# Eighteen more panels of a fused first block by seven products of 128x128x128 instead of eight

## The reference

```
def ssd_shortconv_layer_mixer(x, w_in, conv_w, conv_b, dt_bias, a_log, d_skip, norm_w, sc_conv_w, w_out):
    proj = x @ w_in
...
    return jnp.concatenate([y_ssd.astype(x.dtype), y_sc.astype(x.dtype)], axis=-1) @ w_out
...
    for i in range(DEPTH):
...
        x = layer_norm(ALPHA * x + mix.astype(x.dtype), ln_mix_g[i], ln_mix_b[i])
        x = layer_norm(ALPHA * x + swiglu(x, w_ffn_gate[i], w_ffn_up[i], w_ffn_down[i]), ln_ffn_g[i], ln_ffn_b[i])
        gate = jax.nn.sigmoid(x @ w_ple_gate[i] + b_ple_gate[i])
        x = x + (p[i] @ w_ple[i]) * gate
```

## Time and profile before

| | |
|---|---|
| median of 3 runs (range) | 2324.86 us (2323.5 to 2327.66) |
| the profiled execution's own time | 2325.58 us |
| its span, first to last instruction | 2323.8 us |
| mean granted clock of PE | 0.995 |
| PE busy | 2219.6 us, 96% |
| DVE, POOL, ACT busy | 925.1, 435.6, 382.6 us |

### The profile page before, as it was taken

How to read it: one execution, slowest core, us unless ns; L and a number is a source line. 1 busy time by engine, 2 the same in 40 slices (tenths; PEclk the granted TensorE clock), 3 DMA queues, 4 the chain that set the end, 5 groups by cost and what they waited for, 6 DMA issues and landing times. The chain is left out here.

```text
span 2323.8 us, 35156 instructions
## 1 busy us (share of the span) xinstructions
PE 2219.6 (96%) x14569; PEld 1515.7 (65%) x14569; DVE 925.1 (40%) x1969; ACT 382.6 (16%) x857; POOL 435.6 (19%) x365
## 2 busy tenths in 40 slices
PE   8999999999999998998999999999999999989997
PEld 7888899987799987877633333333333333368786
DVE  4242465645444564626333333333333333352322
ACT  2210121024201023225200000000000000023331
POOL 0120498820088850012000000000000000000000
PEclk9999999999999999999999999999999999999999
DMA  6334754465855454323699999999999999953322
GB/s 264 129 123 145 240 173 162 155 235 179 325 204 166 162 182 171 111 110 146 254 427 427 427 428 428 428 429 408 427 428 427 429 428 428 428 210 131 127 80 84
DMA packets 61011, 619.37 MB, mean 267 GB/s; under 512 B 6784, under 2 KB 8064, under 8 KB 12288
## 3 DMA queue, kind: packets, MB, share of 16 engines
q1 hardware_dynamic: 59184, 611.08, 66.3%
q10 hardware_dynamic: 1712, 6.63, 0.9%
HBM read 616.63 MB, written 1.05 MB: 266 GB/s over the span
## 5 line engine op out<-in xcount | busy, mean ns | idle before, releaser
L2958 PE MATMUL ps<-expert_ring,moe_xg 128*64 128x512 f32 x1280 | 282.1, 593 | 9.9 <-DMA expert_ring<-we_dram 9.5
L3001 PE MATMUL ps<-expert_ring,mix_y 128*64 128x512 f32 x1024 | 228.6, 596 | 10.8 <-DMA expert_ring<-we_dram 10.8
L2958 PEld LDWEIGHTS ps<-expert_ring,moe_xg 128*64 128x64 f32 x1280 | 90.3, 137 | 190.6 <-issue 167.3
L466 PE MATMUL ps<-x_res,ring 128*128 128x256 f32 x896 | 201.1, 382 | 8.8 <-DMA x_res<-x_dram 8.8
L466 PEld LDWEIGHTS ps<-x_res,ring 128*128 128x128 f32 x896 | 169.6, 192 | 33.1 <-DMA ring<-w_in_dram 8.7
L3260 DVE TENSOR_SCALAR mix_y<-ps 128x512 f32<-128x512 f32 x32 | 22.1, 692 | 421.5 <-PE ps L2958 421.5
L2774 POOL COPY unscaled_x<-modulations 128x8 f32<-128x8 f32 x1 | 0.2, 198 | 936.6 <-POOLq L3057 936.6
L2958 PE MATMUL ps<-ring,moe_xg 128*64 128x512 f32 x768 | 168.2, 593 | 0.5 <-DVE moe_xg L2919 0.3
L3001 PEld LDWEIGHTS ps<-expert_ring,mix_y 128*64 128x64 f32 x1024 | 69.8, 137 | 147.2 <-issue 127.5
L466 PE MATMUL ps<-third_h,ring 128*128 128x256 f32 x704 | 160.0, 383 | 1.3 <-DVE third_h L3833 1.0
L625 POOL TENSOR_TENSOR seven_weights<-ring 128x512 f32<-128x512 f32 (+1 forms) x72 | 94.1, 1306 | 326.0 <-DVE seven_x_turned L641 289.2
(11 more groups left out here) (625 smaller groups left out, 3317.7 us busy)
## 6 DMA issues: line engine op xcount, KB each, us to landing
expert_ring<-we_dram SPq DMA_DIRECT2D x144, 2048.0 KB, 22.5
ring<-we_dram SPq DMA_DIRECT2D x48, 2048.0 KB, 24.5
ring<-w_in_dram SPq DMA_DIRECT2D x55, 1024.0 KB, 4.9
ring<-ffn_up_dram SPq DMA_DIRECT2D x44, 1024.0 KB, 5.0
ring<-ada_dram SPq DMA_DIRECT2D x36, 1024.0 KB, 4.9
ring<-w_out_dram SPq DMA_DIRECT2D x16, 1024.0 KB, 4.9
ring<-ffn_dn_dram SPq DMA_DIRECT2D x16, 1024.0 KB, 4.9
ring<-ple_g_dram SPq DMA_DIRECT2D x8, 1024.0 KB, 6.5
```

Source lines behind the costliest of these rows:

```text
L466: mm = pe.matmul(core.ps[:, bank_of[n, c], 0:TOK], w[:, k * PANEL + c * P:k * PANEL + c * P + P], sources[panel](k0 + k), start=(k0 + k == ...
L2958: mm = pe.matmul(ps[out, bank, :], xg[:, j % 4, j // 4, :], w[:, bank * D + at:bank * D + at + 512], start=False, stop=(j == 7))
L3001: mm = pe.matmul(ps[out, 2, :], hidt[:, at_k:at_k + S], w[:, i * D + at:i * D + at + 512], start=False, stop=(k == DT - 1))
```

## The change

Eighteen panels become fast: seven pairs of the input linear (6 to 9, which are z's, and 19 to 21, b's last three), pairs 1 to 3 of the mixer's output linear (two panels each) and pairs 1 to 5 of query, key and value. A linear can now name its fast pairs (`only`). In detail:

- `turn` can run on any engine. The turned x of the input linear is made by POOL at the start (`turn_input`); that of the mixer's output linear by DVE behind tile 43 (`turn_mixed`, twice four operations, into memory of `h_turned`); that of query, key and value by DVE behind tile 119 (`turn_added`).
- POOL's part of the heads has one step for each head from slot 20 on, so that `sums` of panels 6 to 9 stand ahead of them and those of 19 to 21 behind.
- The norm's take of tiles 2 to 5 no longer scales x by ALPHA (`kept`), since `keep` has.

```diff
 def takes(self, name, j):
-        return name in self.first_pair and j >= self.first_pair[name]
+        return name in self.first_pair and j >= self.first_pair[name] and (name not in self.only or j in self.only[name])
...
     def gpsimd(pool):
+        for _ in range(FIRST + 1):
+            yield
         pool.wait_ge(cbm_ready.sem, cbm_ready.at(1))
...
-        yield
+            yield
...
-            if m < 6 and self.alpha != 1.0 and not self.split:
+            if m < 6 and self.alpha != 1.0 and not self.split and m // 2 not in self.kept:
...
+FAST_IN, FAST_OUT = (6, 7, 8, 9, 19, 20, 21), (1, 2, 3)
...
+        out_turned = h_turned[:, :, :, :].rearrange("p c w n -> p (c w n)")[:, 0:2 * 4 * (DT // 2) * P].rearrange(
+            "p (g c w n) -> p g c w n", g=2, c=4, n=P)
+
+        def turned_y(product, k0, p):
+            return out_turned[:, k0 // DT, {5: 0, 7: 1, 6: 2, 4: 3}[product], p, :]
...
+        parts_fast |= {"w_in": (FAST_IN[0], turned_x, None, groups("w_in"), FAST_IN), "qkv": (1, turned_x, None, groups("qkv")),
+                       "w_out": (FAST_OUT[0], turned_y, norms[0].keep, groups("w_out"))}
...
+        def turn_input(pool):
+            clear(pool)
+            pool.wait_ge(core.sem_f.sem, core.sem_f.at(16))
+            seven.turn(pool, seven.groups["w_in", 0], core.x[:, 0:4, :], core.x[:, 4:8, :], *(x_turned[:, i, :, :] for i in (0, 2, 1, 3)))
+
+        def turn_mixed(dve):
+            yield WOUT0 - 1
+            for t in range(WOUT0 - DT, WOUT0):
+                core.wait_tile(dve, t)
+            seven.turn(dve, seven.groups["w_out", 0], y_sc[:, 0:4, :], y_sc[:, 4:8, :], *(out_turned[:, 0, i, :, :] for i in (0, 2, 1, 3)))
+            xd_ready(dve, DT - 1)
+            seven.turn(dve, seven.groups["w_out", DT], xd[:, 0:4, :], xd[:, 4:8, :], *(out_turned[:, 1, i, :, :] for i in (0, 2, 1, 3)))
+
+        def turn_added(dve):
+            yield QKV0 - 1
+            dve.wait_ge(run.x_added.sem, run.x_added.at(DT))
+            seven.turn(dve, seven.groups["qkv", 0], core.x[:, 0:4, :], core.x[:, 4:8, :], *(x_turned[:, i, :, :] for i in (0, 2, 1, 3)))
...
-        linear(core, parts, None, tiles, head=head, act_work=more_loads, pool_work=clear, banks=3,
+        linear(core, parts, None, tiles, head=head, act_work=more_loads, pool_work=turn_input, banks=3,
```

More of the change, by code:

```diff
@@ L575, in __init__ @@
         self.first_pair, self.moving_of, self.keepers = {}, {}, {}
-        for name, (first, moving, keeper, groups) in parts.items():
+        self.only = {}
+        for name, (first, moving, keeper, groups, *only) in parts.items():
             self.first_pair[name], self.moving_of[name], self.keepers[name] = first, moving, keeper
+            if only:
+                self.only[name] = only[0]
             for k0, n in groups.items():
@@ L630, in sums, with turn @@
         pool.tensor_tensor(s4, a12, s2, ALU.subtract).then_inc(summed.sem, 1)
-    def turn(self, dve, n, upper, lower, t1, t2, t3, t4):
+    def turn(self, eng, n, upper, lower, t1, t2, t3, t4):
         turned = self.turned
         b11, b12, b21, b22 = upper[:, :, 0:P], upper[:, :, P:TOK], lower[:, :, 0:P], lower[:, :, P:TOK]
-        dve.tensor_tensor(t1, b12, b11, ALU.subtract).then_inc(turned.sem, 1)
-        dve.tensor_tensor(t3, b22, b12, ALU.subtract).then_inc(turned.sem, 1)
-        dve.wait_ge(turned.sem, turned.at(4 * n + 1))
-        dve.tensor_tensor(t2, b22, t1, ALU.subtract).then_inc(turned.sem, 1)
-        dve.wait_ge(turned.sem, turned.at(4 * n + 3))
-        dve.tensor_tensor(t4, b21, t2, ALU.subtract).then_inc(turned.sem, 1)
+        eng.tensor_tensor(t1, b12, b11, ALU.subtract).then_inc(turned.sem, 1)
+        eng.tensor_tensor(t3, b22, b12, ALU.subtract).then_inc(turned.sem, 1)
+        eng.wait_ge(turned.sem, turned.at(4 * n + 1))
+        eng.tensor_tensor(t2, b22, t1, ALU.subtract).then_inc(turned.sem, 1)
+        eng.wait_ge(turned.sem, turned.at(4 * n + 3))
+        eng.tensor_tensor(t4, b21, t2, ALU.subtract).then_inc(turned.sem, 1)
     def copy_first(self, act, n, one):
@@ L1125, with __init__ @@
 class LayerNorm:
-    def __init__(self, core, run, n, g, b, first, alpha, split, fill):
+    def __init__(self, core, run, n, g, b, first, alpha, split, fill, kept=()):
         self.core, self.run, self.n, self.first, self.alpha, self.fill = core, run, n, first, alpha, fill
@@ L1133, in __init__ @@
         self.sem = dict(zip(names, (*core.shared[28:40], *core.shared[61:63])))
-        self.split = split
+        self.split, self.kept = split, kept
         self.added_before = 0
@@ L1727, in first_block @@
         norms = [LayerNorm(core, run, n, (lambda k, l=l, g=g: core.v(g, l * DT + k)), (lambda k, l=l, b=b: core.v(b, l * DT + k)), first,
-                           alpha, split, mods.fill)
+                           alpha, split, mods.fill, FAST_OUT if first == WOUT0 else ())
                  for n, (g, b, l, first, alpha, split) in enumerate((
@@ L1795, in turned_h @@
             return h_turned[:, {5: 0, 6: 1, 4: 2}[product], k0 // 2 + p, :]
-        turn_order = [("ffn_up0", 0), *(("ffn_dn0", k0) for k0 in range(0, FF_T, KG)), ("ple_g0", 0),
+        out_turned = h_turned[:, :, :, :].rearrange("p c w n -> p (c w n)")[:, 0:2 * 4 * (DT // 2) * P].rearrange(
+            "p (g c w n) -> p g c w n", g=2, c=4, n=P)
+        def turned_y(product, k0, p):
+            return out_turned[:, k0 // DT, {5: 0, 7: 1, 6: 2, 4: 3}[product], p, :]
+        turn_order = [("w_in", 0), ("w_out", 0), ("w_out", DT), ("ffn_up0", 0), *(("ffn_dn0", k0) for k0 in range(0, FF_T, KG)), ("ple_g0", 0), ("qkv", 0),
                       ("ffn_up1", 0), *(("ffn_dn1", k0) for k0 in range(0, FF_T, KG)), ("ple_g1", 0)]
@@ L1821, in turn_h @@
             return program
-        turns = [turn_x("ffn_up0", UP0, norms[0]), turn_h("ffn_dn0", UP0), turn_x("ple_g0", PG0, norms[1]),
+        turns = [turn_mixed, turn_added, turn_x("ffn_up0", UP0, norms[0]), turn_h("ffn_dn0", UP0), turn_x("ple_g0", PG0, norms[1]),
                  turn_x("ffn_up1", UP1, norms[2]), turn_h("ffn_dn1", UP1), turn_x("ple_g1", PG1, norms[3])]
```

## The result

| | before | after |
|---|---|---|
| median (range), 5 runs each | 2327.58 us (2323.5 to 2330.14) | 2336.19 us (2332.43 to 2340.84) |
| the profiled execution's own time | 2325.58 us | 2332.43 us |
| its span | 2323.8 us | 2330.6 us |
| granted clock of PE, mean over that execution | 0.995 | 0.993 |
| PE busy | 2219.6 us | 2212.9 us |

The ratio is 1.0039, 95% interval 1.0025 to 1.0053: slower by 0.25 to 0.53%. The forecast was 2328.9 us with a range of 2321 to 2334, and the median of 2336.19 lies above that range. In ten more runs, beside 27 of the kernel before, the ratio was 1.0033 (1.0020 to 1.0045). The saved work is there, and so are the waits. This is the list of PE's waits in the first 640 us of the changed kernel (total, times, longest), cut at three places; it answers to the earlier trace rows.

A forecast was written before the change was run, and what follows sets the result against it. PE, busy 96% at nearly full clock, bounds the kernel. Saved work of 11.8 us against new waits gave +2.3, one clock fall +1.7: +4.0 on 2325.6 is 2329.6, less 0.7 is 2328.9 us; range 2321 to 2334.

The forecast's parts named there:

- The gain, 18 panels at 6.25 us: In all three linears, 18 panels drop from 6.91 to 6.254 us each, saving PE 11.8 us.
- (a): Input linear, pair 9: PE waits for DVE's copy of the state before the spread, 1.5 us.
- (b): b's last tile: the reciprocal delays panel 21's combining, so PE waits for tile 43, 0.7 us.
- (c): Slot 49, output linear: PE's sum of `ln_offset` waits for DVE's take and addition, slowed by POOL, 2.9 us.
- (d): Slot 51, output linear's norm: the squares' reduction starts later, shifting PE's L1195 and all behind it by 4.0 us.
- (e): Attention: scores, weighing and turning wait for tile 124, ACT's copies and DVE's shift and normalising, together 5.0 us.
- the clock term: PE's clock falls to half once for the new waits at slots 49 and 51 together, adding 1.7 us.
- my own price: Cost of one clock fall: 3.6 us at 0.53 do the work of 1.9 us, so 1.7 us.
- 0.7 us above the median: The profiled execution lay 0.7 us above its three runs' median, so 2329.6 became 2328.9 us.
- the sum without the clock: Saved panel work against the five new waits, before any clock fall: +2.3 us.
- the clock falls at every long new wait: Rival: falls at slot 49, slot 51 and the attention, 3 x 1.7 us, giving 2332.3 us; chance 0.15.

The follow-up runs named there:

- in_only: Kernel before with only the input linear's seven panels made fast: 2322.87 us, ratio 0.9987 to the kernel before.
- warm: Changed kernel plus 13 unread matmuls filling PE's waits at slots 49 and 51: 2330.97 us, ratio 1.0017 to the kernel before.
- shift: Kernel before plus nine unread matmuls at slot 49, making later work start 3.9 us later: 2329.93 us, ratio 1.0011.
- split: Changed kernel with the output linear's layer norm in the down projections' form (first sum over four tiles, squares reduced at slot 49): 2325.28 us, ratio 0.9989.
- out_split: Kernel before with only the output linear's six panels fast, its layer norm in the down projections' form: 2323.88 us, ratio 0.9990.
- best: Changed kernel with query, key and value ordinary and the output linear's norm in the down projections' form: 2325.55 us, ratio 0.9990 to the kernel before.
- qkv_only: Kernel before with only the five panels of query, key and value made fast: 2329.98 us, ratio 1.0016 to the kernel before.
- out_only: Kernel before with only the output linear's six panels made fast, norm unchanged in form: 2334.03 us, ratio 1.0037 to the kernel before.

## Why the prediction was wrong

The waits, which were most of the text, came out. By its points:

- The gain, 18 panels at 6.25 us, came: the first and fourth stretches are within 0.1 us of the saved work less the waits reckoned for them.
- (a) 1.36 us for 1.5. (b) 0.42 for 0.7; the terms listed there add up to 10.1 and not 9.95, which would have made it 0.8. Both waits are where they were said to be, and `in_only` shows that this part of the change gains.
- (c) 3.15 for 2.9, and for the reason given, DVE slowed by POOL. DVE's timeline of the changed kernel has the take at 1.07 and the addition at 1.37 us while POOL sums for a later panel; the same take at slot 51, with POOL idle, takes 0.42:

```profile
228.40 0.55 DVE L661 TENSOR_TENSOR seven_stage<-seven_part,ps 128x384 f32<-128x384 f32 x1 [1.24 <-PE ps L430]
228.99 1.07 DVE L1161 TENSOR_TENSOR x_res<-x_res,seven_stage 128x256 f32<-128x256 f32 x1
230.09 1.37 DVE L1242 TENSOR_TENSOR ln_offset<-ln_offset,x_res 128x256 f32<-128x256 f32 x1
...
246.95 0.42 DVE L1161 TENSOR_TENSOR x_res<-x_res,seven_stage 128x256 f32<-128x256 f32 x1
```

- (d) The waits are 1.57 + 1.96 = 3.53 us, where PE was to get the squares 4.0 us later than before. That was a little too large, and the wait ahead of L445 gave 0.5 back (0.90 for 1.36), which I had not counted.
- (e) The six new waits are 4.42 us in sum for 5.0, each within 0.2 of its term. The stretch is 1.75 longer for 1.7 reckoned.
- **The step that failed is the clock term: "I take one fall for the two: +1.7".** In both profiles of the changed kernel (c) and (d) have a fall each, and the unchanged second down projection has a third that the kernel before escaped. On the profiled execution, 2332.43 for 2329.6, 2.8 us were missing: one more fall in the stage, 1.7 by my own price, and the 1.4 us of the unchanged part make 3.1, less what (d) and (e) were too large.
- The other 4.5 us of the miss are in the last step, "0.7 us above the median". It carried an offset over from three runs of the kernel before. Against the five runs of the result (median 2327.58) the same execution was 2.0 us below the median, and against the 91 later ones 1.1 below. So 2.7 us of the miss are in the median of before that I started from, and the forecast change was 4.0 us where 8.2 to 8.6 were measured. The rest is the clock again: the profiled run after had 0.993 where the 15 have 0.9918, and their median is 3.3 us above it.

How much is clock in all can be read from the runs. Over 218 runs of these kernels, each kernel's own mean taken off, the time falls by 1.77 us for each 0.001 of mean clock (correlation -0.89). The 91 runs of before and the 15 of after, grouped by clock (medians):

```
clock    0.991   0.992   0.993   0.994   0.995
before   2332.3  2331.6  2329.5  2329.7  2326.6
after    2336.5  2335.7  2332.0  2331.4  2327.7
runs     1, 4    4, 3    10, 2   17, 2   33, 1
```

At one and the same clock the changed kernel is 1 to 4 us slower, though most of these medians of it are of one to three runs. The means of all runs, 2334.98 and 2327.09 us, are 7.9 apart. Of this the difference in clock, 0.9947 - 0.9918 = 0.0029, is 5.1 us by the slope, and 2.7 are left, near what the sum without the clock had said (+2.3). I had put 1.7 for the clock. The 5.1 is an estimate from a correlation; by profile, 2.65 us of it stand in the output linear's stage (`warm`). The rival nearest to it was the second, "the clock falls at every long new wait", at 2332.3 us, and even that is below the measured median; it counted falls of the changed places only.

What is shown: that the output linear's stage pays 2.65 us to two falls, which are gone when its waits are filled (`warm`); that added work of 3.9 us without a wait does not lower the mean clock (`shift`); that without the three waits the stage is back at its old time or 0.9 us under it, and 7 to 8 us below the changed kernel's (`split`, `out_split`, `best`). Not shown is what lowers the clock elsewhere: the attention's short waits bring no fall there, yet `qkv_only` has a mean of 0.9934, and single places of unchanged work fall in one kernel and not in another (`best`). So the cause of the other half of the 5.1 us stays open.

## What to carry to other kernels

When PE is the bound and every panel is made shorter, the work that hung on "one more tile" loses its cover. Look at each place where two woven steps come to stand next to each other, and give the early step a form that needs only older tiles, as the split norm does. Price a new wait of PE with its length and with the clock that it may cost, for the whole program and not only for its place, and take the clock from many runs, not from one profile. A part that gains by itself (the input linear) is worth separating from one that loses, and a repaired part is to be compared with that one too, not only with the kernel before: `best` is not shown to beat `in_only`.

## What the runs showed of the hardware

- A wait of PE of the same length is followed by half clock in one execution and not in another: 3.15 us at L1174 with two matmuls at 1.22 us in the changed kernel and at 0.70 in `out_only`; 2.35 us at L430 likewise (8 matmuls in 1.73 us in the changed kernel, 1.16 behind 2.37 us in the kernel before). Half clock also came within 4 us behind a wait of 2.03 us (`split`, `out_split`, `best`).
- Half clock came at 1129 to 1136 us of `best`, where no wait of PE in 1110 to 1140 was longer than 0.4 us, and did not come in the attention, with waits of 0.5 to 0.9 us six times in 35 us (granted 1.00).
- The mean granted clock of the same program differs from run to run, 0.991 to 0.996 for the kernel before, and the time with it, 2332.3 us (one run) to 2324.7 us (median of 26). That is as large as the effect of the change.
- A 128x256 addition of two SBUF operands on DVE took 0.42 us with POOL idle, 1.07 and 1.37 us with POOL adding weight blocks of 128x512 from SBUF. Both ended 0.3 us after POOL's instruction did (230.06 after 229.77, 231.46 after 231.18).
